# The hybrid layer by two heads a step with features on partitions, and a router whose scale is put on the logits

## The reference, cut to what matters

```
h = rms_norm_2(x, g_mix)
qa, ka, va, qb, kb, vb, qi, ki, wi, ga, gb = split(h @ w_in)     # 6 x 512, 512, 64, 8, 1024, 1024
o_a = 8 causal heads of 64 (rope on qa, ka)
score = sum over 8 index heads of wi * relu(qi . ki)             # rope on qi, ki
o_b = 8 causal heads of 64 over the 64 best-scored keys of each query
mixed = sigmoid(ga) * (o_a @ w_proj_a) + sigmoid(gb) * (o_b @ w_proj_b)
x = x + mixed @ w_out
xt = rms_norm_2(x, g_ffn)
g_logit = xt @ w_group + b_group ; e_logit = xt @ w_expert + b_expert   # 4 groups of 8 experts
# best group, its two best experts, gate = softmax weight of the group * the two probabilities, normalised
x = x + sum over 2 experts of gate * (silu(xt @ w1[e]) * (xt @ w3[e])) @ w2[e]
```

## Time and profile before

| | |
|---|---|
| median of 3 runs | 1419.42 us (1415.28 to 1419.5) |
| profiled execution, time | 1416.78 us |
| its span | 1415.0 us |
| PE busy in the span | 1330.8 us (94%) |
| DVE, ACT, POOL busy | 518.4, 553.7, 567.4 us (37 to 40%) |
| mean granted TensorE clock | 0.978 |
| HBM read | 339.10 MB, 240 GB/s over the span |

### The profile page before, as it was taken

How to read it: one execution, slowest core, us unless ns; L and a number is a source line. 1 busy time by engine, 2 the same in 40 slices (tenths; PEclk the granted TensorE clock), 3 DMA queues, 4 the chain that set the end, 5 groups by cost and what they waited for, 6 DMA issues and landing times.

```text
span 1415.0 us, 19947 instructions
## 1 busy us (share of the span) xinstructions
PE 1330.8 (94%) x7717; PEld 970.4 (69%) x7717; DVE 518.4 (37%) x1323; ACT 553.7 (39%) x852; POOL 567.4 (40%) x132
## 2 busy tenths in 40 slices
PE   6999999999977899999999998889999999999996
PEld 5767999998866799998877775664544454444442
DVE  2333444443462544445345454251111121111112
ACT  4553655555573555554454664111111111111112
POOL 5622788885743288886567652200000000000000
PEclk9999999999998999999999998999999999999998
DMA  8631665655541176654445530659999999999995
GB/s 264 215 90 60 188 199 179 196 191 168 189 120 60 55 237 186 200 184 157 140 158 159 169 120 29 263 212 400 423 422 422 423 423 422 423 423 423 423 422 206
DMA packets 164260, 341.21 MB, mean 241 GB/s; under 512 B 11001, under 2 KB 113754, under 8 KB 139610
## 3 DMA queue, kind: packets, MB, share of 16 engines
q1 hardware_dynamic: 164186, 340.18, 65.4%
HBM read 339.10 MB, written 1.05 MB: 240 GB/s over the span
## 4 chain that ended last, share of the span: by engine, by line
PE 81%; DMA 7%; DVE 6%; ACT 2%; SPq 2%; issue 1%; POOL 1%; ACTq 0%; DVEq 0%
PE bank L624 16%; PE bank L626 16%; PE bank L625 16%; PE bank L1114 12%; PE bank L1138 6%; DMA ring<-in_w 6%; PE bank L1065 3%; PE bank L723 3%; SPq L559 2%; PE bank L757 2%; PE bank L634 2%; PE bank L1095 1%; POOL low L586 1%; PE bank L653 1%; PE bank L749 1%
## 5 line engine op out<-in xcount | busy, mean ns | idle before, releaser
L586 POOL TENSOR_TENSOR low<-raw,high 128x2048 fp32r<-128x2048 f32 (+4 forms) x128 | 567.2, 4455 | 342.8 <-ACT high L1183 342.8
L624 PE MATMUL bank<-xh,high 128*128 128x256 f32 x872 | 243.9, 280 | 6.0 <-POOL low L586 3.8
L1183 ACT ACTIVATE high<-raw 128x2048 fp32r<-128x2048 f32 (+4 forms) x128 | 235.2, 1846 | 18.9 <-PE bank L624 9.1
L626 PE MATMUL bank<-xh,low 128*128 128x256 f32 x872 | 242.5, 278 | 0.0
L625 PE MATMUL bank<-xl,high 128*128 128x256 f32 x872 | 242.5, 278 | 0.0
L1114 PE MATMUL bank<-ring,room 128*64 128x512 f32 x768 | 228.3, 595 | 6.5 <-DMA ring<-in_w 4.8
L624 PEld LDWEIGHTS bank<-xh,high 128*128 128x128 f32 x872 | 164.6, 189 | 10.0 <-POOL low L586 4.2
L624 PE MATMUL bank<-high,xh 128*128 128x512 f32 (+4 forms) x400 | 158.2, 395 | 10.5 <-DVE xl L1580 4.7
L625 PEld LDWEIGHTS bank<-xl,high 128*128 128x128 f32 x872 | 164.8, 189 | 0.8
L626 PEld LDWEIGHTS bank<-xh,low 128*128 128x128 f32 x872 | 164.9, 189 | 0.0
L626 PE MATMUL bank<-high,xl 128*128 128x512 f32 (+4 forms) x400 | 153.8, 385 | 0.0
(11 more groups left out here) (210 smaller groups left out, 1777.2 us busy)
## 6 DMA issues: line engine op xcount, KB each, us to landing
ring<-in_w SPq DMA_DIRECT2D x144, 1024.0 KB, 24.0
raw<-in_ffn_w_up SPq DMA_DIRECT2D x88, 512.0 KB, 5.0
room<-in_w SPq DMA_DIRECT2D x24, 1024.0 KB, 21.0
xspare<-in_w SPq DMA_DIRECT2D x24, 1024.0 KB, 25.9
raw<-in_ffn_w_down SPq DMA_DIRECT2D x44, 512.0 KB, 3.9
raw<-in_w_in SPq DMA_DIRECT2D x44, 512.0 KB, 4.5
raw<-in_diff_w_qkv SPq DMA_DIRECT2D x24, 512.0 KB, 4.6
raw<-in_mla_w_o SPq DMA_DIRECT2D x8, 512.0 KB, 5.0
```

What stands on the lines that cost most here:

```text
L586: pool.tensor_tensor(low[:, p % PARTS, 0:n], raw[:, p % RING, 0:n], high[:, p % PARTS, 0:n], ALU.subtract).then_inc(low_ready, 1)
L624: first = pe.matmul(out_, a[0], b[0], start=start, stop=False)
L626: return first, pe.matmul(out_, a[1], b[0], start=False, stop=stop)
L1183: act.activation(high[:, p % PARTS, 0:n], raw[:, p % RING, 0:n], ACT.Copy).then_inc(high_ready, 1)
```

## The change

- Attention works on two heads a step: 8 steps (`duo`) of 2 heads (j = 0, 1 on the two halves of the array). Scores of j go to bank j, transposes to bank 2+j, the two outputs to the two halves of bank 4. The probabilities have six places, two of them in `gpost`.
- The gates are by feature, in 8 pieces of 256 columns (`GATES` says in which step). The scale of the token, which was a scalar of the row, becomes a row: PE multiplies ones by a diagonal (`row`), and DVE multiplies the gate by it in PSUM. ACT takes tanh(x/2) in place of sigmoid; the halves come in at the end.
- The projections are by feature. Those of the b heads start after the attention with three of four k tiles. `mixed` is so already transposed: `mix_t` and its 16 transposes, and the sum in SBUF, are gone. `mixed @ w_out` waits group by group.
- `qi`, `ki` and `wi` are one product of 584 columns in three pieces (256 + 328 columns a matmul). `qa` follows before the transposes of `qi`. The index products are rectified in place in PSUM, and DVE reads them there.
- Router: `xn` is only gained, tile by tile, without the scale; the logits get the scale. DVE chooses by the logits themselves, with max and match_replace, in 13 instructions; the exponentials and gates are made later, between the first selection and the first gather's copy. ACT scales `xn` before the gather. `keep_clock(12)` ahead of the transposes is gone, and the other is 12 matmuls, not 24.
- SP: slot 0's first half waits for the last probabilities, its second for the last output; the load of g_final moves behind all of the layer's pieces and waits for a transpose.

```diff
-STAGES = {"mla_att": (MH, 1), "diff_att": (DH, 2), "hyb_att": (16, 1)}
+STAGES = {"mla_att": (MH, 1), "diff_att": (DH, 2), "hyb_att": (8, 2)}
+GATES = {1: [0, 1], 2: [2, 3], 3: [4], 4: [5], 5: [6], 6: [7]}
...
# PE
-            columns("qi")
-            columns("ki")
-            rotated("qi")
+            by_token(G["qi"], W["qi"], X, [3, 3, 2], [256, 328])
+            pe.wait_ge(diag_ready, 1)
+            b = begin(G["row"])
+            for t in range(NT):
+                ins = pe.matmul(b[:, t * P:t * P + P], cs[:, C_ONE:C_ONE + P], diag[:, t], start=True, stop=True)
...
             columns("qa")
...
+                if s == 0:
+                    by_token(G["vb"], W["vb"], X, [4, 4], [512])
+                    rotated("kb")
+                for n in GATES.get(s, []):
+                    two_heads(G[f"g{n}"], W["gates"] + n)
+                if s in (8, 10):
+                    n = s // 2 - 4
+                    for st_ in range(4):
+                        moved(pe, A_["hyb_att"][2][st_])
+                    pe.wait_ge(low_ready, W["pa"] + n + 1)
+                    features(G[f"pa{n}"], W["pa"] + n, (hh, hl))
...
+            for s in range(steps + 3):
...
+                    for j in range(2):
+                        b = begin(sc[s, j])
+                        for t in range(NT):
+                            ins = pe.matmul(b[:, t * S:t * S + S], q[64 * j:64 * j + 64, m, t * P:t * P + P],
+                                            k[64 * j:64 * j + 64, m, :], start=True, stop=True)
...
+                hyb_beside(s)
+                if s >= 3:
...
+                    for j in range(2):
+                        for k in range(NT):
+                            ins = pe.matmul(b[64 * j:64 * j + 64, 0:S],
+                                            (va, vb)[x // 4][:, k, 128 * (x % 4) + 64 * j:128 * (x % 4) + 64 * j + 64],
+                                            pT[:, j, k, :], start=k == 0, stop=k == NT - 1)
...
+                if 2 <= s < steps + 2:
...
+                    for j in range(2):
+                        b = begin(tr[x, j])
+                        for k in range(NT):
+                            for t in range(NT):
+                                ins = pe.transpose(b[:, k * S + t * P:k * S + t * P + P],
+                                                   duo(x, j, t, k * P, P), ident)
...
-                    transposes(G["mix_t"] + 2 * t + q, [siga[:, t, P * k:P * k + P] for k in range(4 * q, 4 * q + 4)])
-            square_out("hyb_o", W["wout"], X)
-            keep_clock(12, begin(G["x5"]), hl)
-            x_transposed("x5", 5)
+            for n in range(2):
+                pe.wait_ge(low_ready, W["pb"] + n + 1)
+                for m in (0, 2):
+                    begin(G["pb"] + 2 * n + m // 2)
+                    tile_of(G["pb"] + 2 * n, parts(W["pb"] + n, 4, 512), ob, m, 0, 3)
+            moved(pe, ou[7])
+            for n in range(2):
+                features(G["pb"] + 2 * n, W["pb"] + n, ob, opened=True)
+            for m in range(4):
+                moved(pe, G["pb"] + m)
+                by_token(G["hyb_o"], W["wout"] + m, ((xh[:, 4:8], xl[:, 4:8]), (hh, hl))[m // 2], [2], [512, 512],
+                         lambda c, t: 2 * t + c, 2 * m, KT, x_from=4 * (m // 2))
...
-            keep_clock(24, b, hl)
+            keep_clock(12, b, hl)
             pe.wait_ge(mask_ready, 1)
...
             moved(pe, G["pos"])
+            pe.wait_ge(rows_scaled, NT)
# ACT
+            used = [2, 4, 6, 7, 8, 9, 10, 10, 11, 11, 12]
+            for s in range(steps + 3):
+                if s < steps:
+                    (four exponentials)
+                split(W["vb"] + used[s] + (1 if s < 3 else 2))
...
+                for n in GATES.get(s - 1, []):
+                    act.wait_ge(gate_scaled, n + 1)
+                    act.activation(tanh_of[n // 4][:, 512 * (n % 4):512 * (n % 4) + 512], bank[BANK[g]][:, :], ACT.Tanh,
+                                   scale=0.5).then_inc(bank_moved[BANK[g]], 1)
+                if s >= 3:
+                    (high part of output s - 3)
+                if 2 <= s < steps + 2:
+                    (two copies of the transposes s - 2)
# DVE, step s
+                (two scores with their mask, two minima)        # s < 8
+                (gates of step s - 1 by the scale row, in PSUM)
+                (low part of output s - 4)
+                (duo s - 1: wait for its exponentials, reciprocal, four products)
+                (top-64: two rounds a step in steps 0 to 3; gates of o_a in steps 9 and 11)
# SP
-                if c == 0:
-                    sp.wait_ge(mixed_ready, 1)
+                if c == 0 and a == 0:
+                    sp.wait_ge(probs, MH + DH + 8)
+                elif c == 0:
+                    full(sp, A_["hyb_att"][2][7])
                 elif c < 3:
                     sp.wait_ge(low_ready, W["end"] - RING + 2 * (c - 1) + a + 1)
```

More of the change, by code:

```diff
@@ L135, in attention, with pairs @@
                 ou[s - 3] = ou[s - 4] if paired and s % 2 == 0 else one(banks and banks[2])
-    def at_step(n, name, count):
-        return lambda s: groups(name, count) if s == n else None
+    def pairs(name, beside):
+        steps, two = STAGES[name]
+        sc, tr, ou = A[name] = {}, {}, {}
+        for s in range(steps + 3):
+            if s < steps:
+                for j in range(two):
+                    sc[s, j] = one(j)
+            beside(s)
+            if s >= 3:
+                ou[s - 3] = one(4)
+            if 2 <= s < steps + 2:
+                for j in range(two):
+                    tr[s - 2, j] = one(2 + j)
     for name, n in [("x0", 4), ("mla_down", 4), ("mla_t", 2), ("mla_t2", 2)]:
@@ L1025, in _, with features @@
-            projected("b", 1)
-            for t in range(NT):
-                pe.wait_ge(mixed_ready, t + 1)
-                for q in range(2):
-                    transposes(G["mix_t"] + 2 * t + q, [siga[:, t, P * k:P * k + P] for k in range(4 * q, 4 * q + 4)])
-            for g in range(4):
-                moved(pe, G["mix_t"] + g)
-            square_out("hyb_o", W["wout"], X)
-            keep_clock(12, begin(G["x5"]), hl)
-            x_transposed("x5", 5)
+            def features(g, p, x, opened=False):
+                w = parts(p, 4, 512)
+                for m in range(4):
+                    if m % 2 == 0 and not opened:
+                        begin(g + m // 2)
+                    tile_of(g, w, x, m, 3 if opened and m % 2 == 0 else 0, 4)
+                    if m % 2:
+                        end(last_of[0], g + m // 2)
+                owed[0] += 1
@@ L1282, in attention @@
                         between(s)
-                    if s == heads and name in ("mla_att", "hyb_att"):
+                    if s == heads and name == "mla_att":
                         load_table(ACT.Abs_reciprocal_sqrt)
@@ new lines, in _ @@
+                if s >= 3:
+                    g, x = ou[s - 3], s - 3
+                    high_part(g, (hh, xh)[x // 4][:, x % 4, :], bank[BANK[g]][:, 0:S])
+                if 2 <= s < steps + 2:
+                    for j in range(2):
+                        g = tr[s - 2, j]
+                        copy(g, pT[:, j].rearrange("p k q -> p (k q)"), bank[BANK[g]][:, :])
+            heads_done[0] += steps
+            load_table(ACT.Abs_reciprocal_sqrt)
+            split(W["pb"] + 3)
+            mixed = [(y[0][:, 4:8], y[1]) for y in ((xh, hh), (xl, hl))]
@@ L1952, in _ @@
-            low_tiles("mix_t", TILE_HALVES, 4)
+                if s in (9, 11):
+                    for x in range(2):
+                        g = G[f"pa{(s - 9) // 2}"] + x
+                        m = s - 9 + x
+                        moved(dve, G[f"g{m}"])
+                        full(dve, g)
+                        y = tanh_of[0][:, 512 * m:512 * m + 512]
+                        dve.scalar_tensor_tensor(y, y, 1.0, bank[BANK[g]][:, :], ALU.add,
+                                                 ALU.mult).then_inc(bank_moved[BANK[g]], 1)
@@ L2012, in _ @@
[L2012 to L2018 removed]
+            for t in range(NT):
+                ins = dve.max(top_of[:, t, :], e_of[:, t, :])
@@ L2079, in one_round @@
                 pair(base + (NP - 1), NP - 1, 1, last=True)
-            select(0, 0)
+            select(0, 0, gates=False)
+            dve.wait_ge(logits_exp, 4)
+            link(dve.tensor_tensor(e_exp, e_exp, mask, ALU.mult))
+            link(dve.tensor_reduce(r_scale, e_exp, AX, ALU.add))
+            link(dve.tensor_tensor(r_scale, r_scale, r_sums[:, 0:2], ALU.mult))
+            link(dve.reciprocal(r_scale, r_scale))
+            for t in range(NT):
+                ins = dve.tensor_scalar(gate[:, t, :], e_exp[:, t, :], r_scale[:, t:t + 1], None, ALU.mult)
+            link(ins)
+            link(dve.tensor_copy(gpair, gate[:, :, 0:2]))
             take(0)
```

463 lines of the change are left out of this document (255 added, 208 removed).

## The result

The changed kernel takes 1396.2 us (median of 4 runs, 1392.2 to 1398.0), the kernel before 1419.2 in the same comparison: ratio 0.9849, 95% interval 0.9825 to 0.9872 (the two medians by themselves give 0.9838, inside it). Measured once more beside the experiments it was 1394.7 and 0.9849 (0.9831 to 0.9867). So it is faster by 23 us, a little less than half of the 47.8 forecast, and 1396.2 lies above the range's end of 1388.

A forecast was written before the change was run, and what follows sets the result against it. The weight stream sets the program's end, a constant after the first weight use, so time before 951.7 us counts in full. Gains 5.1 + 33.2 + 9.5 = 47.8 us gave 1369.0 profiled, median 1371.5; forecast 1364 to 1378, range 1362 to 1388.

The forecast's parts named there:

- The end follows the first use of a weight: Expert stage: the weight stream ends a constant after the first use of a weight, if the filling is done.
- The filling is done in time: Before the expert stage: the first filling of the 8 weight slots ends before the first use, by 3 us.
- Index part: 672.1 to 710.7 us, fused qi and ki products: net gain 5.1 us, bounds 2.5 and 6.5.
- Attention: 757.5 to 924.2 us, to the last w_out matmul: 166.7 down to 133.5, gain 33.2, bounds 19 and 38.
- Stalls by following the chain: Attention: PE's waits in step 8, step 9, w_out's third piece and steps 4 to 6, together 4.8 us.
- The clock term: Attention: half clock around the holes costs 1.8 us, against 9 us of missing clock before.
- Router: 924.2 to 951.7 us: PE goes on 9.5 us earlier, bounds 6 and 10.3.
- Outputs that don't pair (1): Attention: two heads' outputs run one after another, 8 steps x 1.0 us, 1379; chance 15%.
- ScalarE and VectorE as the bound (2): Attention steps 3 to 8: ACT and DVE set the pace, 2.5 us more a step, 15 us, 1386; chance 11%.
- the splits late (4): Attention: a piece's low comes only in the step using it, 18.2 us a step for 8.8, 1446; chance 4%.
- the filling (3): Router: slot filling takes its place as limit, 3 to 8 of the 9.5 us are lost, 1377; chance 7%.
- the change did what it says (5 out): Rival 5, whole kernel: a fill or wait pins the stream at 955, within 4 us of 1419; chance 3%.

The follow-up runs named there:

- e6: Kernel before with the router's part of the change alone, index part and attention as before: 1401.6 us, ratio 0.9896.
- e10: Kernel before with the index part of the change alone: 1415.0 us, ratio 1.0006.
- e11: e10 with one bank of the round skipped, so that kb keeps banks 4 and 5 as in the kernel before: 1413.0 us, ratio 0.9976.
- e7: e4 with one more edit of the bank plan, moving the pa, pb and w_out products to other banks: 1366.6 us, ratio 0.9643.
- e4: Changed kernel with vb copies in step 0, two output banks, early one-operation mask, vb and kb_t banks moved, tanh before splits: 1368.6 us, ratio 0.9660.
- e3: Changed kernel with selection rounds 3, 3, 2 in steps 0 to 2 and the mask made in step 2 by one operation: 1389.5 us, ratio 0.9808.
- e9: Changed kernel with the mask made by one operation instead of two, in its old place in step 3: 1390.3 us, ratio 0.9828.

## Why the prediction was wrong

**The end follows the first use of a weight: right.** SP's first load behind it came 17.8 us earlier (955.37 to 937.58), the last half of w3 18.0 us earlier (the earlier trace rows to 1369.08), the span is 19.4 shorter. **The filling is done in time: right, just so.** Of the 3 us to spare, 0.9 were left by an estimate: 295 of 422 GB/s over the 3 us from 938. If the router got faster still, this would probably come next; no run shows it.

**Prices: right.** Scores of 8 in 1.14, outputs of 8 in 1.09, the transposes 1.09. Outputs of the two heads pair.

**Index part: 4.5 for 5.1, in part by luck, with a side effect that was missed.** At one clock the gain is 2.6 us (35.3 to 32.7), at the forecast's bound of 2.5. The 18.1 us that the forecast took for `qi` and `ki` before held 1.7 of half clock, and it took 1 us more for the clock behind them: in `e6` they took 16.4 (668.03 to 684.38), with the same 72-column matmuls and no loss of clock, so the gain was not the edit's alone, and these matmuls alone aren't the cause of the lower clock. `e10` and `e11` show that where the round of banks stands after this part decides 6 us of the next stage by the traces, 4 by the ratios. In the changed kernel the `row` group fills the tenth place, but `vb` went from banks 4 and 5 to 5 and 6, which costs the same wait, 3.43 where it was 1.14.

**Attention: wrong, and this is the failed step: "Stalls by following the chain".** It gave 4.8 us of stalls and 1.8 of half clock; they were 25.7 and about 11.5 (164.1 - 126.9 - 25.7), of which 11.2 stand behind the five holes. The 126.9 of PE's own work stands: in `e7` PE is busy for 127.8 and the stretch is 132.07, the forecast 133.5, with 2.9 us of the stalls that the forecast listed (low part of output 3 in step 8: 1.7 for 1.9; step 9's copies: 0.8 for 1.4; w_out's piece: 0.4 for 0.8; steps 4 to 6: none for 0.7), and 1.4 in step 1, for a weight's low part, that it had not listed. The median of `e7`, 1366.6, is within the forecast of 1364 to 1378, so what failed is the plan of banks and queues that the change brought, not the work it saves. So the chain was followed for data and engines, and right there. It wasn't followed for the bank of each new group: who had it last, which instruction empties it, and what stands ahead of that one in its queue. The row was even quoted: VectorE's 4655 ns for the mask entered as 0.7, because only the first of its two operations was priced (the second took 0.69 before and 4.95 now) and the low part that the next output needs wasn't seen behind it.

**The clock term followed from the holes.** `vb`'s 48 products took 12.8 us after the 3.43 hole and 11.3 in `e4` without it; gates 0 and 1 took 13.2 after the 8.99 hole and 11.2 in `e4`. So these two cost 1.5 and 2.0 us more at the lower level; behind the last two, where short groups and waits follow, the missing clock is 2.9 and 3.1.

**Router: right in kind, 11.4 for 9.5, above its bound of 10.3.** The products end 6.4 behind w_out (forecast 7.1), the mask 9.3 (10.5), and the 12 fillers took 2.98 us where 4.2 had been taken from 24 that ran partly at half clock. By the forecast's own figures the fillers end 9.8 earlier (945.3 to 935.5), and the second tile's `xn` ends at 928.5, not 928.7. The 11.4 sets a trace at 1.00 against one at 0.87; with the changed router at 0.75 (`e3`) it would be 7.1.

**The rivals.** Outputs that don't pair (1) are out by their price; ScalarE and VectorE as the bound (2), and the splits late (4), are refuted by `e4` (but for the 1.4 us in step 1); the filling (3) lost nothing; the change did what it says (5 out). None of them was the mechanism that came, and the lower bound of the attention term, 19, was made of rivals 1 and 2 alone, so the range ended 8 us short.

## What to carry to other kernels

For every group that a change puts into a PSUM bank, write down the bank's last holder, the instruction that empties it and the queue ahead of that instruction; a change of the plan is priced by that table, not by the engines' load. A cut that alters how many banks a round-robin uses moves every later group: compare the neighbours' banks before and after. And the releaser that a profile names for a hole is only the last link (step 4's bank): look at what made it late before moving it.

## What the runs showed of the hardware

- VectorE's operations that make the mask, with all operands in SBUF, stood still while GpSimd worked: 4.66 us before, then 2.54, 4.95, 2.83, 2.78 and 3.80 (changed kernel twice, `e9`, `e3`, `e4`) for 512 columns, each ending a few tenths of a us after an instruction of GpSimd (0.3 before, 0.5 for the 4.95 and in `e9`); the one that had no GpSimd beside it took 0.69 (L1924 of before). Operations with an input in PSUM took 0.64 to 0.69 beside GpSimd. Not all in SBUF are held: in `e4` the products by a column's scalar with a sum took 0.48 for 256 columns beside it (804.05, GpSimd busy from 798.87 to 812.6), as they do without. The Trainium skill (SBUF — State Buffer, SBUF: two separate sides) calls it a lock on a shared port pair, held for the whole instruction, which takes in operations with two SBUF inputs and the two-port modes; these rows agree. The 2.54 and the 4.66 were operations with one input, so by the page they would have run in such a mode.
- Two heads' outputs, eight matmuls on the two column halves with head 0's four first in program order, took 1.09 us, where four took 1.08. The Trainium skill (TensorE: Matmul & The Clock Gate, Part 3) has matmuls in strict order, but also measures three tiles on different columns at 2.38 times the speed of one after another; this price agrees with the second, and shows that head by head order doesn't keep column halves from running beside each other. The rule that the forecast made of it, outputs one after another, doesn't hold.
- tanh between exponentials: ScalarE's timeline of the changed kernel has a table load at 754.68, ahead of the first exponential, and the next at 884.06, behind the last tanh, none between (the kernel before, with sigmoid, has nine from 758.27 to 838.41). So it is as the Trainium skill (ScalarE: Activation LUTs, Table sets) says.
